# Second mixer: the head norm from one full-width product with ones, root and reciprocal on every channel, in place of 16-row sums and their spreading

## The reference, cut to what matters

```python
o = o * lax.rsqrt(jnp.mean(o * o, axis=-1, keepdims=True) + EPS)
o = o * head_g.astype(f32).reshape(A_HEADS, A_VDIM)
o = o.reshape(B_, T, A_WIDTH) * jax.nn.silu(og.astype(f32))
```

## Time and profile before

| What | Value |
|---|---|
| median of 3 runs | 2919.57 us (2918.3 to 2920.6) |
| profiled execution, own time | 2917.1 us |
| its span | 2915.0 us |
| TensorE matmul busy | 2828.1 us, 97% of the span |
| VectorE busy | 2001.1 us, 69% |
| ScalarE busy | 1013.5 us, 35% |
| GpSimd busy | 1122.9 us, 39% |
| mean granted TensorE clock | 0.994 |

### The profile page before, as it was taken

The page is one execution under the profiler, slowest core; times in us unless marked ns, Lnnn a source line. Parts: engine busy times, 40 slices in busy tenths (PEclk is TensorE's granted clock), DMA queues, the critical chain, the costliest instruction groups (busy, mean ns, idle before and its releaser), DMA issues. The chain is left out here.

```text
span 2915.0 us, 55296 instructions
## 1 busy us (share of the span) xinstructions
PE 2828.1 (97%) x21636; PEld 2460.4 (84%) x21636; DVE 2001.1 (69%) x3205; ACT 1013.5 (35%) x1492; POOL 1122.9 (39%) x873
## 2 busy tenths in 40 slices
PE   7999999999999999998999999999999999999998
PEld 6787888787888888877999999999978888888887
DVE  6898865568777777777467768774436676666755
ACT  3231544434333333344223233224323333332333
POOL 0001432317656556550222232221314655555552
PEclk9999999999999999999999999999999999999999
DMA  4111000322111121124111111123421112111112
GB/s 130 46 51 37 3 3 26 107 75 63 47 53 53 47 61 47 47 81 138 44 52 57 33 52 32 51 64 112 142 85 44 51 47 61 47 54 50 47 47 87
DMA packets 205344, 173.09 MB, mean 59 GB/s; under 512 B 10573, under 2 KB 182053, under 8 KB 204773
## 3 DMA queue, kind: packets, MB, share of 16 engines
q1 hardware_dynamic: 198245, 161.88, 18.0%
q10 hardware_dynamic: 6912, 8.52, 0.8%
HBM read 149.27 MB, written 21.10 MB: 58 GB/s over the span
## 5 line engine op out<-in xcount | busy, mean ns | idle before, releaser
L3103 DVE TENSOR_TENSOR tokens_x<-ffn_acc,tokens_x 128x512 f32<-128x512 f32 x450 | 301.8, 686 | 66.9 <-PE ffn_acc L2659 66.7
L3920 PE MATMUL mix_e<-blk_hi,mix_w_hi 128*128 128x348 f32 (+3 forms) x1056 | 346.0, 328 | 1.8 <-DVE blk_lo L3058 1.2
L3920 PE MATMUL mix_e<-blk_lo,mix_w_hi 128*128 128x348 f32 (+3 forms) x1056 | 339.2, 321 | 0.0
L3920 PE MATMUL mix_e<-blk_hi,mix_w_lo 128*128 128x348 f32 (+3 forms) x1056 | 338.0, 320 | 0.0
L2642 PE MATMUL ffn_out<-ffn_T,ffn_w12h 128*128 128x512 f32 x1008 | 313.1, 392 | 5.6 <-POOL ffn_w12l L2520 3.5
L2659 PE MATMUL ffn_acc<-blk_hi,ffn_hid_hi 128*128 128x512 f32 x900 | 309.5, 393 | 1.3 <-issue 1.3
L3489 POOL TENSOR_TENSOR mix_w_lo<-mix_raw,mix_w_hi 128x1024 fp32r<-128x1024 f32 x44 | 109.0, 2477 | 367.1 <-ACT mix_w_hi L3524 367.1
L2520 POOL TENSOR_TENSOR ffn_w03l<-ffn_r,ffn_w03h 128x512 fp32r<-128x512 f32 x126 | 193.2, 1534 | 122.9 <-ACT ffn_w03h L2871 119.3
L2642 PEld LDWEIGHTS ffn_out<-ffn_T,ffn_w12h 128*128 128x128 f32 x1008 | 188.4, 189 | 45.8 <-POOL ffn_w12l L2520 4.4
L2520 POOL TENSOR_TENSOR ffn_w12l<-ffn_r,ffn_w12h 128x512 fp32r<-128x512 f32 x114 | 167.7, 1481 | 106.3 <-ACT ffn_w12h L2871 104.4
L3920 PEld LDWEIGHTS mix_e<-blk_hi,mix_w_hi 128*128 128x128 f32 x1056 | 198.4, 188 | 6.6 <-issue 2.0
(11 more groups left out here) (538 smaller groups left out, 7024.1 us busy)
## 6 DMA issues: line engine op xcount, KB each, us to landing
ffn_r<-ffn_up SPq DMA_DIRECT2D x88, 256.0 KB, 3.0
mix_raw<-w_in SPq DMA_DIRECT2D x44, 512.0 KB, 3.8
ffn_r<-w_up SPq DMA_DIRECT2D x88, 256.0 KB, 3.0
ffn_room<-ffn_down SPq DMA_DIRECT2D x20, 512.0 KB, 4.0
ffn_room<-w_down SPq DMA_DIRECT2D x20, 512.0 KB, 4.0
proj_w_raw<-w_in_first SPq DMA_DIRECT2D x19, 512.0 KB, 3.8
branch_gates<-proj SPq DMA_DIRECT2D x16, 520.0 KB, 4.7
wout_raw<-w_out SPq DMA_DIRECT2D x16, 512.0 KB, 3.9
```

Source lines behind the costliest of these rows:

```text
L3103: return vec.tensor_tensor(dst, accs[t % len(accs)], dst, ALU.add)
L3920: last = nc.tensor.matmul(dst[:, 0:m], a[n % 2][:, kd, :], b[:, kd, c:c + m], start=kd == 0 and part_ == 0, stop=kd == KD - 1 and part_ == 2)
```

## The change

The window and expand matrices go. One matrix `head_ones`, 128 by 128, with ones where row and column belong to the same head, takes their place: one product per third of the columns (`head_sums`) gives the sum of squares of a head on all its 64 channels at once. The root (ScalarE) and the reciprocal (VectorE) are then taken on all 128 partitions and all 1040 columns, in thirds, in an SBUF tile `factor`, and the spreads are gone. `inverse` and `finish` of a third now stand together at the end of VectorE's iteration, one third in each of the slots `8(j+1)+1` to `8(j+1)+3`, and for the last pair after all four `split_ob`.

```diff
-        spreads = [(f"spread{b}", u // 8 - 1) for b in range(3)] if u % 8 == 1 and u > 8 else []
+        sums = [(f"sum{b}", u // 8 - 1) for b in range(3)] if u and u % 8 == 0 else []
...
-                    sp.dma_start(window[:], const_of(consts, "head_window")).then_inc(consts_landed, 16)
-                    sp.dma_start(expand[:], const_of(consts, "expand")).then_inc(consts_landed, 16)
+                    sp.dma_start(head_ones[:], const_of(consts, "head_ones")).then_inc(consts_landed, 16)
...
-            def deviation(j):
-                for x in range(2):
-                    last = activation(std[row_set(x), :], bank("sum", j)[row_set(x), 0:GROUP], ACT.Sqrt, scale=1.0 / N,
-                                      bias=eps[row_set(x), :])
+            def deviation(j, b):
+                c, m = THIRDS[b]
+                await_piece(act, f"sum{b}", j)
+                if j:
+                    act.wait_ge(finished, j)
+                activation(factor[:, c:c + m], bank(f"sum{b}", j)[:, 0:m], ACT.Sqrt, scale=1.0 / N, bias=eps[:]).then_inc(
+                    taken(f"sum{b}", j), 1)
...
-                vec.reciprocal(inv[:], std[:]).then_inc(inv_ready, 1)
+            def inverse(j, b):
+                c, m = THIRDS[b]
+                await_taken(dve, f"sum{b}", j)
+                vec.reciprocal(factor[:, c:c + m], factor[:, c:c + m]).then_inc(inv_ready, 1)
...
-                vec.scalar_tensor_tensor(o[:, j % 2, cs], bank(f"spread{b}", j)[:, 0:cs.stop - cs.start], hg, o[:, j % 2, cs],
-                                         ALU.mult, ALU.mult).then_inc(taken(f"spread{b}", j), 1)
+                dve.wait_ge(inv_ready, 3 * j + b + 1)
+                vec.scalar_tensor_tensor(o[:, j % 2, cs], factor[:, cs], hg, o[:, j % 2, cs], ALU.mult, ALU.mult).then_inc(
+                    scaled, 1)
...
-                if spreading:
-                    finish(u // 8 - 1, 0)
...
-                if spreading:
-                    finish(u // 8 - 1, 1)
...
-                if spreading:
-                    finish(u // 8 - 1, 2)
...
-                if u and u % 8 == 0:
-                    inverse(u // 8 - 1)
+                if u > 8 and 1 <= u % 8 <= 3:
+                    inverse(u // 8 - 1, u % 8 - 1)
+                    finish(u // 8 - 1, u % 8 - 1)
...
-            inverse(PAIRS - 1)
             for row in range(2, 4):
                 split_ob(row)
             for b in range(3):
+                inverse(PAIRS - 1, b)
                 finish(PAIRS - 1, b)
...
+            def head_sums(j, b):
+                c, m = THIRDS[b]
+                pe.wait_ge(squared, j + 1)
+                dst = start_piece(pe, f"sum{b}", j)
+                end_piece(mm(dst[:, 0:m], head_ones[:], sf[:, 1, c:c + m], start=True, stop=True), f"sum{b}", j)
```

More of the change, by code:

```diff
@@ L3294, in mixer_pieces @@
         dense = pieces_of_slot(u)
-        spreads = [(f"spread{b}", u // 8 - 1) for b in range(3)] if u % 8 == 1 and u > 8 else []
-        order += [("dense", dense[0])] + spreads[0:1]
+        sums = [(f"sum{b}", u // 8 - 1) for b in range(3)] if u and u % 8 == 0 else []
+        order.append(("dense", dense[0]))
         if u % 8 == 0:
             order += [(f"vt{b}", u // 8) for b in range(3)]
-        order += [("kt", u), ("dense", dense[1])] + spreads[1:2]
-        if u and u % 8 == 0:
-            order.append(("sum", u // 8 - 1))
-        order += spreads[2:3] + [("dense", p) for p in dense[2:]]
+        order += [("kt", u), ("dense", dense[1])] + sums[0:2] + [("dense", dense[2])] + sums[2:3]
+        order += [("dense", p) for p in dense[3:]]
     tail = list(range(pieces_of_slot(H * UNITS)[0], 3 * CHUNKS2))
-    order += [("dense", p) for p in tail[:4]] + [("sum", PAIRS - 1)] + [("dense", p) for p in tail[4:]]
-    order += [(f"spread{b}", PAIRS - 1) for b in range(3)]
+    order += [("dense", p) for p in tail[:4]] + [(f"sum{b}", PAIRS - 1) for b in range(2)]
+    order += [("dense", tail[4]), ("sum2", PAIRS - 1)] + [("dense", p) for p in tail[5:]]
     assert sum(name == "dense" for name, _ in order) == 3 * CHUNKS2 and sorted(BLOCKS2) == list(range(CHUNKS2))
@@ L3339, in mixer2 @@
         masks = s.sb("masks", [P, 8, C1])
-        window = s.sb("window", [P, CONST_AT["head_window"][1]])
-        expand = s.sb("expand", [P, CONST_AT["expand"][1]])
+        head_ones = s.sb("head_ones", [P, P])
+        factor = s.sb("factor", [P, T2])
         rate = s.sb("rate", [P, 64])
@@ L3667, in scalar @@
                 activations(u)
-                for p in dense[2:]:
+                evacuate(dense[2])
+                if u and u % 8 == 0:
+                    deviation(u // 8 - 1, 2)
+                for p in dense[3:]:
                     evacuate(p)
@@ L3677, in scalar @@
             evacuate(tail_pieces[3])
-            deviation(PAIRS - 1)
+            deviation(PAIRS - 1, 0)
+            deviation(PAIRS - 1, 1)
             branch_weight()
@@ L3681, in scalar @@
             split_ob(3)
-            for p in tail_pieces[4:]:
+            evacuate(tail_pieces[4])
+            deviation(PAIRS - 1, 2)
+            for p in tail_pieces[5:]:
                 evacuate(p)
@@ L4028, in update @@
                           skip_group_check=True)
-            def sums_of(j):
+            def head_sums(j, b):
+                c, m = THIRDS[b]
                 pe.wait_ge(squared, j + 1)
[L4032 to L4043, removed]
-                    rows, r = summed_at(m)
-                    last = mm(dst[:, n * GROUP:(n + 1) * GROUP], expand[rows, r * P:(r + 1) * P], inv[rows, :], start=True,
-                              stop=True)
-                end_piece(last, f"spread{b}", j)
+                dst = start_piece(pe, f"sum{b}", j)
+                end_piece(mm(dst[:, 0:m], head_ones[:], sf[:, 1, c:c + m], start=True, stop=True), f"sum{b}", j)
             pe.wait_ge(join.drained, NT)
@@ L4091, in tensor @@
             dense(tail_pieces[3])
[L4092 to L4093 removed]
+            head_sums(PAIRS - 1, 0)
+            head_sums(PAIRS - 1, 1)
+            dense(tail_pieces[4])
+            head_sums(PAIRS - 1, 2)
+            for p in tail_pieces[5:]:
                 dense(p)
[L4095 to L4096 removed]
     return Stage(sync, gpsimd, tensor, scalar, vector), First(first_load, first_hi, first_dense, second_dense, rest_of_second)
```

45 lines of the change are left out of this document (12 added, 33 removed).

## The result

The changed kernel takes 2931.33 us (median of 8 runs, 2926.24 to 2937.22) against 2918.41 of the kernel before (8 runs): ratio 1.0046, 95% interval 1.0037 to 1.0055. It is slower by 13 us, 0.46%; the forecast was 2921.0 and its range ended at 2927.0. The prediction was wrong.

The account below looks back on a forecast made before the run. TensorE was taken to bound the slots and VectorE's path the barrier: -4.7 + 5.9 + 0.3 = +1.5 us, so 2921.0 us against the median 2919.57, no measurable change; range 2916.5 to 2927.0.

Parts of the forecast that it names:

- TensorE's side: Slots: sums and spreads lose 3.62 us a pair, three new products cost 2.05; three pairs save 4.7 us.
- The reciprocals: VectorE's wider reciprocals: 2.30 us for 348 columns, 2.28 for 344, 6.88 a pair instead of 0.96.
- Rival A: Slower because wide reciprocals are dearer and VectorE becomes the bound: at 3.3 us a third, +8.1, 2927.7 us; chance 0.14.
- The last pair: Reciprocals and products after the last `split_ob`, on VectorE's path to the barrier, move the block's end by +5.9 us.
- 3.35 for the last: Last pair's final third on VectorE: reciprocal and two products, without overlap but four columns fewer, 3.35 us against 3.38.
- Rival B: In the tail the reciprocals vanish in VectorE's idle time; only -4.4 us is left, 2915.2 us; chance 0.07.
- Does VectorE still answer in time in the slots?: Nine iterations get 3.45 us more on VectorE; it fits, barely, with +0.3 us (0 to 2) for small misses.
- 0.24 is left: Slot 19: VectorE's first-tile mask 2.34 us late against 2.58 to spare before TensorE's outputs, so 0.24 us remains.
- the delays don't add up: In the slots VectorE waits for the second tile's scores behind the first mask, so it is back in step.
- Rival D: GpSimd holds up `finish`, now reading two SBUF tensors, up to 1.3 us in three or four slots: +4, 2925; chance 0.09.
- The restart: TensorE's clock after about 10 us idle at the barrier: -1.5 to +1.5 us, taken as nothing.

Follow-up runs that it names:

- the last pair as before: Changed kernel with pair 3's norm in the old form (16-row sums, one reciprocal, spreads): 2925.6 us, ratio 1.0021 to the kernel before.
- the early reciprocals: Changed kernel with the last pair's first two reciprocals moved ahead of the third `split_ob`: 2925.7 us, ratio 1.0032 to the kernel before.
- the third piece behind `state`: Changed kernel with the first three pairs' third reciprocal and finish moved behind the next iteration's second-tile `state`: 2925.0 us, ratio 1.0028.
- low halves narrowed: Changed kernel with GpSimd computing only 64 of 1024 columns of the weights' low halves from block 10 on: 2920.2 us, ratio 1.0008.
- the finer pieces with the new last pair: Changed kernel with the first three pairs' reciprocals ending iterations 1, 4, 6 of 8 and finishes 2, 5, 7: 2920.0 us, ratio 1.0009.

## Why the prediction was wrong, point by point

**TensorE's side held.** Sums and spreads at 3.62 us a pair came off: slot 9 is shorter by the 1.50 of its spreads. The three products cost slot 8, which lost 2.14, 17.31 - 15.24 = 2.07 against 2.05 taken (slot 0 of this profile is 15.24). The gain is 5.2 us in the slots where nothing waits, against 4.7.

**The reciprocals held.** 2.320 us for 348 columns, 2.296 for 344, against 2.30 and 2.28. The repeat count of 8 in the Trainium skill ("VectorE: DVE Perf Modes", First, the fixed hardware budget), read as 8 cycles an element, would have made it 2.9, an estimate; the measurement decides against that reading. Rival A, dearer reciprocals, is out.

**The last pair held.** +6.1 us against +5.9; the difference is the hand-over from a reciprocal to its product, 0.10 and not 0.03, three times. (The prediction's "3.35 for the last" third is a slip: its own terms give 3.44, and only with that do the three make its sum of 10.2. Measured are 3.48, 3.48 and 3.52.) TensorE's idle time is 11.5 us and not "about 10", since the 1.4 us that it no longer works there were left out of it. That VectorE's order sets the barrier is shown by the runs with the last pair as before and with the early reciprocals. Rival B is out.

**"Does VectorE still answer in time in the slots?" is the step that failed.** It put +0.3 us (0 to 2) where TensorE waited 8.2 us, and some 1.5 to 4 more where the clock fell. Two errors are in it. The first is the deadline. I wrote that after `forget` and `double` comes "`state`, where it waited, then `mask` of the first tile, for which TensorE's outputs wait", and read the margin at the mask. In three slots of four that is right. In the fourth TensorE's tail-tile outputs wait for that `state` itself, a microsecond behind the update; the third piece stood in front of just this one in all three pairs. The rows that I took as typical, slots 19 and 20, showed the mask's margin, 2.6 and 2.9 us, and not this one's. In iteration 12 it was nil; in 20 and 28 VectorE had 1.10 and 1.55 us of idle time ahead of `state`, against a piece of 3.45. The run with the third piece behind `state` shows it.

Nor were the two rows typical of the mask. In slots 26, 27 and 28 of the kernel before it ended only 0.43, 1.11 and 1.45 us ahead of the outputs, and in slots 26 and 27 TensorE then waited for it. Slot 26, before and after:

```profile
1901.67 0.45 DVE L3793 TENSOR_TENSOR mix_work<-mix_work 64x64 f32<-64x64 f32 x2
1902.55 0.30 PE L4010 MATMUL mix_out<-mix_work,mix_vt 128*64 128x128 f32 x1
```

```profile
1910.04 0.45 DVE L3791 TENSOR_TENSOR mix_work<-mix_work 64x64 f32<-64x64 f32 x2
1910.75 0.29 PE L4000 MATMUL mix_out<-mix_work,mix_vt 128*64 128x128 f32 x1 [0.58 <-DVE mix_work L3791]
```

The second pair shows a slip in the sum too: outputs that wait for the mask start 0.26 us behind its end (1910.75 - 1910.49), so 0.26 of each margin can't be used, and the "0.24 is left" of slot 19 was nothing.

The second is "the delays don't add up". I took it that VectorE waits for the second tile's scores in each slot and so starts afresh, with GpSimd's hold-ups unchanged. In the kernel before it did wait (1.26 us in slot 10, 1.33, 1.35 and 1.40 in 11, 18 and 19). In the changed kernel there is no such wait in slots 10, 11, 18, 19, 26 and 27, so a delay is handed on to the next slot. With low halves narrowed there is one of 0.9 to 1.1 us in each of these six, and TensorE waits nowhere. Slot 10 before, changed, and with low halves narrowed:

```profile
1639.52 0.69 DVE L3778 TENSOR_TENSOR mix_work<-mix_sc,mix_masks 128x512 f32<-128x512 f32 x1 [1.26 <-PE mix_sc L3982]
```

```profile
1644.87 0.68 DVE L3776 TENSOR_TENSOR mix_work<-mix_sc,mix_masks 128x512 f32<-128x512 f32 x1
```

```profile
1641.46 0.69 DVE L3777 TENSOR_TENSOR mix_work<-mix_sc,mix_masks 128x512 f32<-128x512 f32 x1 [1.13 <-PE mix_sc L3973]
```

The hold-ups were there before as well, 2.2 us each in slots 10 and 11, with idle time behind them to take them up; with that gone they lengthen the path. In iterations 9 to 11 they now fall on `finish` itself (2.08, 1.40 and 1.45 us), in 18 and 19 on other instructions (2.2 and 2.1). Rival D had the mechanism and too small a price: it charged the hold-up where `finish` meets GpSimd and left out that it takes away the last of what was to spare. That the two together make the loss, and not either one, no rival said.

**The restart** taken as nothing: between the first product of the ending and the 300th behind it lie 48.8 to 50.2 us in all fourteen profiles, 49.8 in the changed kernel's and 48.8 before. What this goes by is how long the granted clock stays at 0.50 behind the restart: 3.0 us before, 5.2 in the changed kernel, 6.0 where the distance was 50.2, half a microsecond of distance for each microsecond of it. It doesn't go by the length of the idle time: with 4.4 us ahead the clock stayed low for 3.0, 4.8, 4.9 and 5.7 us, with 11.5 for 3.5 to 6.0. So the restart gave this one pair of profiles 1.0 us of difference, and no price of the longer idle time can be told from such a scatter.

What stays open is a part of the size. Slots and end give 9.6 us, the medians 12.9. In the five kernels of the table without a wait of over 0.1 us, the median over the kernel before lies 0.4 under to 1.6 us over what the two stretches give; in the changed kernel (both times) and the three variants that keep its waits of slots 11 and 19, it lies 2.3 to 4.1 us over, counted without half speed; the other three lie between 3.7 under and 2.8 over. That fits a clock that falls behind the long waits, at 1.5 to 4 us an execution, but the intervals are 2.5 to 4.5 us wide either way, so it isn't shown, and how often the clock falls in timed runs was not seen, only in profiles: behind the wait of slot 11 in four of the five that have one of 1.5 us or more there (the changed kernel once of twice, and three of its variants), behind that of slot 19 in three of five.

## What to carry to other kernels

When work is moved onto an engine "with slack", list every consumer that waits for something behind the insertion, in every kind of iteration (first, last, tail tile), and read the margin at each; the smallest counts, not the typical one. Idle time is used up once: pieces in successive iterations share it, and stalls that fell into it before come out as delays. A gain of 5 us on the bound engine became a faster kernel only once the added work had been moved or cut finer in the slots, and taken off the last stretch before the barrier, in whole or in part.

## What the runs showed of the hardware that was not expected

A wait of 1.5 to 2.8 us of TensorE in the middle of dense work went with a stretch of granted clock 0.50, from late in the wait or just behind it, in 8 of the 11 such waits in the profiles: 3.4 us long in six, 6.8 in two (at the 2.8 us of slot 19). Slot 12 then took 16.3 us instead of 14.8, and slots 19 and 20 together 37.3 instead of 34.7. So such a wait costs its own length and in some executions 1.4 to 2.5 us more. Whether it also makes a kernel's times scatter is not shown: the changed kernel's runs span 11 us (2926.2 to 2937.2), but those of the finer pieces with the new last pair, which has no such wait, span 9.5.

A reciprocal (one SBUF tensor in, 2.30 us) kept its speed while it ran beside a GpSimd subtraction for 0.65 us; the same subtraction, of 2.40 us, held the next product of two SBUF tensors for 1.45 us of its 2.02.
